# Thirty-two modulation chunks later in a two-block kernel, and two FFN groups that take the contraction by turns

## What is computed

```python
# first block
mod = silu(c) @ w_ada + b_ada                       # 2048 -> 6 * 2048
sh_a, sc_a, gt_a, sh_f, sc_f, gt_f = split(mod, 6)
h = rmsnorm(x, g_pre_attn) * (1 + sc_a) + sh_a
...                                                  # attention on h @ w_in, then w_out
x = x + gt_a * rmsnorm(mix @ w_out, g_post_attn)
h = rmsnorm(x, g_pre_ffn) * (1 + sc_f) + sh_f
f = (silu(h @ w_gate) * (h @ w_up)) @ w_down         # 2048 -> 5632 -> 2048
x = x + gt_f * rmsnorm(f, g_post_ffn)
# second block
shift, scale, gate = split(silu(c_2) @ w_ada_2 + b_ada_2, 3)
h = rms_norm(x, norm1_w) * (1 + scale) + shift
...                                                  # h @ w_in_2, mLSTM, convolution, merged
x = x + gate * (merged @ w_out_2)
return rms_norm(x, normf_w)
```

## Time and profile before

| | |
|---|---|
| median of 3 runs | 2268.4 us (2267.27 to 2268.63) |
| the profiled execution, its own time | 2267.31 us |
| its span | 2265.5 us |
| PE busy | 2235.4 us, 99% |
| DVE busy | 1815.3 us, 80% |
| ACT busy | 1117.6 us, 49% |
| moved by DMA | 598.47 MB, mean 264 GB/s |
| granted clock of PE, mean over the span | 0.998 |

### The profile page before, as it was taken

The page is one execution under the profiler, slowest core; times in us unless marked ns, Lnnn a source line. Parts: engine busy times, 40 slices in busy tenths (PEclk is TensorE's granted clock), DMA queues, the critical chain, the costliest instruction groups (busy, mean ns, idle before and its releaser), DMA issues.

```text
span 2265.5 us, 26257 instructions
## 1 busy us (share of the span) xinstructions
PE 2235.4 (99%) x10314; PEld 1904.2 (84%) x10314; DVE 1815.3 (80%) x2448; ACT 1117.6 (49%) x1473; POOL 14.7 (1%) x31
## 2 busy tenths in 40 slices
PE   9999999999999999999999999999999999999998
PEld 4378888888888888888888888888888888888887
DVE  6788998988889888987675677998878796565885
ACT  5356677564444444544464444444445544454453
POOL 0000000000000000000000000000000000000000
PEclk9999999999999999999999999999999999999999
DMA  9978888888889888898746655556666657655553
GB/s 401 419 291 318 300 341 339 332 319 300 295 318 330 296 296 297 317 352 337 279 164 217 206 209 200 195 200 214 218 218 218 211 197 276 211 202 201 197 205 130
DMA packets 87757, 598.47 MB, mean 264 GB/s; under 512 B 10145, under 2 KB 10209, under 8 KB 16593
## 3 DMA queue, kind: packets, MB, share of 16 engines
q1 hardware_dynamic: 85538, 588.95, 71.2%
q0 software_dynamic: 1664, 7.19, 0.9%
q10 hardware_dynamic: 432, 0.66, 0.1%
HBM read 594.62 MB, written 2.13 MB: 263 GB/s over the span
## 4 chain that ended last, share of the span: by engine, by line
PE 81%; DVE 12%; DMA 3%; issue 2%; ACT 2%; DVEq 0%; ACTq 0%
PE PS L1185 20%; PE PS L1201 16%; PE PS L1210 16%; PE PS L1202 16%; PE PS L1190 10%; DVE LO L1657 4%; DVE RAW L1667 2%; DMA RAW<-in_w_mod 2%; DVE R L1699 2%; DMA RAW<-in_w_first 1%; ACT HI L673 1%; DVE X L1748 0%; PE PS L1362 0%; PE PS L1581 0%; PE PS L1554 0%
## 5 line engine op out<-in xcount | busy, mean ns | idle before, releaser
L673 ACT ACTIVATE HI<-RAW 128x1024 fp32r<-128x1024 f32 x784 | 825.2, 1056 | 991.2 <-PE PS L1210 610.6
L1657 DVE TENSOR_TENSOR LO<-RAW,HI 128x1024 fp32r<-128x1024 f32 x784 | 956.0, 1224 | 368.3 <-ACT HI L673 364.4
L1201 PE MATMUL PS<-HI,XH 128*128 128x512 f32 x2080 | 800.1, 385 | 3.4 <-ACT HI L673 2.4
L1202 PE MATMUL PS<-HI,XL 128*128 128x512 f32 x2080 | 789.3, 379 | 0.0
L1210 PE MATMUL PS<-LO,XH 128*128 128x512 f32 x2080 | 536.6, 380 | 1.5 <-DVE LO L1657 1.4
L1201 PEld LDWEIGHTS PS<-HI,XH 128*128 128x128 f32 x2080 | 393.6, 189 | 62.7 <-DVE XL L1930 3.5
L1210 PEld LDWEIGHTS PS<-LO,XH 128*128 128x128 f32 x2080 | 393.4, 189 | 58.5 <-DVE LO L1657 2.7
L1202 PEld LDWEIGHTS PS<-HI,XL 128*128 128x128 f32 x2080 | 393.7, 189 | 53.7
L1185 PE MATMUL PS<-HI,XH 128*128 128x512 f32 x1056 | 314.8, 380 | 1.9 <-DVE XL L1771 1.3
L1185 PE MATMUL PS<-HI,XL 128*128 128x512 f32 x1056 | 314.1, 379 | 0.0
L1190 PE MATMUL PS<-LO,XH 128*128 128x512 f32 x1056 | 272.7, 379 | 0.0
(11 more groups left out here) (266 smaller groups left out, 895.0 us busy)
## 6 DMA issues: line engine op xcount, KB each, us to landing
RAW<-in_w_second SPq DMA_DIRECT2D x208, 1024.0 KB, 4.9
RAW<-in_w_mod SPq DMA_DIRECT2D x144, 1024.0 KB, 6.0
RAW<-in_w_ffn SPq DMA_DIRECT2D x88, 1024.0 KB, 5.0
RAW<-in_w_first SPq DMA_DIRECT2D x64, 1024.0 KB, 5.8
RAW<-in_w_down SPq DMA_DIRECT2D x44, 1024.0 KB, 5.2
...
R<-mod_rows POOLq DMA_DIRECT2D x3, 1024.0 KB, 7.6
X<-in_x SPq DMA_DIRECT2D x2, 1024.0 KB, 8.6
```

The source lines that it names most:

```text
L673: act.activation(HI[:, (it["half"] + hf) % HLS, :], whole, ACT.Copy).then_inc(s.hi_ready, 1)
L1201: pe.matmul(PS[:, bank + u, :], XH[:, 2 * n + kk, rows], hi, start=start and kk == 0, stop=False)
L1202: pe.matmul(PS[:, bank + u, :], XL[:, 2 * n + kk, rows], hi, start=False, stop=False)
L1657: dve.tensor_tensor(LO[:, slot, :], RAW[:, it["slot"], hf * 1024:(hf + 1) * 1024], HI[:, slot, :].bitcast(F32), ALU.subtract).then_inc(s.l ...
```

## The change

Five things are altered.

1. Eight A are taken out of first: those behind chunks 22, 25, 28, 31, 34, 37, 40 and 43. It holds 68 then; the FFN's shift and scale are ready for pairs 0 to 4 alone when the FFN starts.
2. The FFN's groups 0 and 1 take the contraction by turns: five chunks of group 0, five of group 1, three of group 0, three of group 1. So pairs 5, 6 and 7 are first used at halves 20, 22 and 24. PE transposes pairs 3 to 7 behind halves 2 to 6; ACT copies pairs 5 to 7 from PSUM to SBUF unmodulated (keep_turned, ahead of which stands the copy of halves 8 to 10); their modulation stands at halves 11, 17 and 22. Twelve A, four for each of the three pairs, stand behind the FFN's chunks 1 to 10, two behind chunks 7 and 9. ffn has 40 A in all, down 20.
3. The sixteen A of the last gate are done in second, one behind each of chunks 166 to 181 (halves 332 to 363). For them POOL loads c_2's row into C_ROW once more and ACT takes its silu at half 330.
4. Group 0's evacuation comes at half 29, and its transposes at halves 30 to 37, two to a half.
5. The warm-up matmuls at the start are 22 and 14 small ones (run_warm, 128 columns in float32) in place of 20 and 16 (first_warm, second_warm); the memset of HI for them is gone.

The diff, cut to the core:

```diff
-ADA_BEHIND = list(range(20, 64))
-ADA_ORDER = [*range(62), *range(64, 78), 62, 63, 78, 79, *range(80, 144)]
-ADA_WITH_FFN = 76
+ADA_BEHIND = [c for c in range(20, 64) if c not in range(22, 46, 3)]
+
+LATE_PAIRS = (5, 6, 7)
+ADA_ORDER = [*range(58), *range(64, 74), *(a for n in LATE_PAIRS for a in (48 + 2 * n, 49 + 2 * n, 64 + 2 * n, 65 + 2 * n)),
+             *range(80, 144)]
+ADA_WITH_FFN = 68
+ADA_LAST_GATE = 128
...
+MODULATED_AT = {6: 3, 8: 4, 11: 5, 17: 6, 22: 7}
...
+def ffn_chunks():
+
+    first = [(g, k) for ks in (range(0, 2 * LATE_PAIRS[0], 2), range(2 * LATE_PAIRS[0], NK, 2)) for g in range(2) for k in ks]
+    return first + [(g, k) for g in range(2, 11) for k in range(0, NK, 2)]
...
 def ffn_body():
     body = []
-    for c in range(11 * NK // 2):
-        body.append(("W", c // 8, 2 * (c % 8)))
-        if 5 * c // 11 != 5 * (c + 1) // 11 or c in (1, 3, 40, 42):
+    for c, (g, k) in enumerate(ffn_chunks()):
+        body.append(("W", g, k))
+        body += [("A",)] * (c in range(1, 11)) + [("A",)] * (c in (7, 9))
+        if c > 10 and 28 * (c - 11) // 77 != 28 * (c - 10) // 77:
             body.append(("A",))
...
-        if k < 36 and k % 3:
+        if k < 40 and k % 2:
             body.append(("A",))
+def second_body():
...
+            if 166 <= 4 * g + k // 4 < 182:
+                body.append(("A",))
...
             pool.wait_ge(s.hat_ready, 4)
+            pool.dma_start(NORMF, normf_w_2[None, :].to_broadcast([P, D])).then_inc(s.normf_in, 16)
+            pool.wait_ge(s.group_out, left(PROJ_B - 1))
+            pool.dma_start(C_ROW, c_rows[1:2, :].to_broadcast([P, D])).then_inc(s.c_2_in, 16)
             gate_rows(2, GG2)
-            pool.dma_start(NORMF, normf_w_2[None, :].to_broadcast([P, D])).then_inc(s.normf_in, 16)
...
+            def keep_turned(n):
+
+                no = turn_no(0, n, 0)
+                act.wait_ge(s.pair_t, no)
+                act.activation(as_turned(n), turned_to(0, n, (0, 1)), ACT.Copy).then_inc(s.pair_out, 1)
...
+                late = t == 0 and n in LATE_PAIRS
+                if late:
+                    act.wait_ge(s.mod_ready, 10 + LATE_PAIRS.index(n))
+                    act.wait_ge(s.pair_out, no)
...
-                    if h in (7, 9, 11, 13, 15):
-                        modulate(0, (h - 1) // 2, (0, 1))
+                    if h in MODULATED_AT:
+                        modulate(0, MODULATED_AT[h], (0, 1))
                     if h >= 4:
                         hi_half(sec, 0, it, hf)
...
+                    if h in (8, 9, 10):
+                        keep_turned(h - 3)
...
+                if h == 330:
+                    act.wait_ge(s.c_2_in, 32)
+                    act.activation(C_ROW, C_ROW, ACT.Silu).then_inc(s.cact_ready, 1)
...
-            pe.wait_ge(s.dve_chain, 5)
-            first_warm()
+            run_warm(7, 22)
...
-            second_warm()
+            run_warm(0, 14)
...
-                    if h in (3, 5, 7, 9, 11):
-                        turn_pair(0, (h + 3) // 2, (0, 1), 5 + (h > 3))
+                    if 2 <= h < 7:
+                        turn_pair(0, h + 1, (0, 1), 5 + (h > 2))
...
-                if a == MOD_AT[0] + 31:
-                    modulation(2, 1, 14, 16, ADA_WITH_FFN + 4)
+                for i, n in enumerate(LATE_PAIRS):
+                    if a == MOD_AT[0] + NK + 2 * n + 1:
+                        modulation(2 + i, 1, 2 * n, 2 * n + 2, ADA_WITH_FFN + 4 * i + 4)
```

113 lines of the change are left out of this document (61 added, 52 removed).

## The result

| | before | after |
|---|---|---|
| median of the runs that stood side by side | 2267.84 us (2265.84 to 2268.63, 4 runs) | 2284.0 us (2280.35 to 2285.32, 4 runs) |
| ratio after to before, 95% interval | | 1.0066 (1.0054 to 1.0078) |
| the profiled execution, its own time | 2267.31 us | 2284.29 us |
| its span | 2265.5 us | 2282.5 us |
| granted clock of PE, mean over the span | 0.998 | 0.995 |

The change makes the kernel slower by 0.66%, some 15 us. The prediction had the side right and the size wrong: 2274.6 us, range 2269 to 2279. The change was run a second time in the study (run e5): ratio 1.0059 (1.0046 to 1.0071).

The account below looks back on a forecast made before the run. TensorE (PE), busy for 99% of the span, bounds the kernel, so only waits change. Terms -1.5 + 4.8 + 1.7 + 1.2 = +6.2 us take 2267.3 to 2273.5, median 2274.6; range 2269 to 2279.

Parts of the forecast that it names:

- Term 1: Beside attention: two PE waits for DVE, 1.24 and 0.23 us, go with the A taken out; -1.5 us.
- Term 2: Start of the FFN: DVE's work and round trips with ACT make half 22 start later than 514.77; +4.8 us.
- DVE's list of 51.5 us: FFN's start, ahead of half 22's LO: 12 A, 18 LO, XL of pairs 3 to 6, three modulations.
- the round trips: FFN's start: DVE's modulation, then ACT's pair and HI; 2.0 us for pairs 5 and 6 together, 2.65 for pair 7.
- so they are just hidden: FFN's start: at 422 GB/s the seventeenth load lands at 507.5, half 20 needs it at 509.6; no cost.
- Term 3: PE's clock at the FFN's start: one fall to about half for 3.4 us after a wait; +1.7 us, bounds none or two.
- Term 4: Second block, halves 351 to 369: DVE's work for the last gate outruns its 7.0 us stock; +1.2 us, 0 to 3.
- land late once: Second block, upper bound of 3 us: loads of W and A, two in 5.2 us, come late one time.
- Terms at nothing: Small warm-ups (0 to +1 us), group 0's evacuation, two f_turn to a half, POOL's row, gate_rows: no cost.
- The loads set the pace: Rival, FFN's start: loads at 360 GB/s, half 22 late by 8.1 instead of 4.8; +9.5 in all, 2277.9 us; chance 0.12.

Follow-up runs that it names:

- e4: Smaller version of the change: four A leave first, pairs 6 and 7 late, silu at half 26, last gate's A in down; 2266.05 us, ratio 0.9991.
- e7: Changed kernel, loads of the FFN's first twelve A cut to 512 of 2048 columns, DVE's work whole; 2281.28 us, ratio 1.0053.
- e2: Changed kernel with pair 7's modulation and XL one half later, at half 23; 2280.86 us, ratio 1.0055.
- e6: Changed kernel, DVE taking 64 of 2048 columns of each of the FFN's first twelve A, loads whole; 2275.5 us, ratio 1.0035.
- e9: Changed kernel, the FFN's first twelve A loading 512 columns and DVE taking 64 of them; 2269.65 us, ratio 1.0005.
- e1: Changed kernel with silu of c_2's row behind half 26 of the FFN instead of half 20; 2282.59 us, ratio 1.0059.
- e12: Changed kernel with the last gate's A back in down, silu of c_2's row at half 26, pair 7 at half 23; 2277.27 us, ratio 1.0040.
- e14: Kernel before with only the last gate's sixteen A moved into the second block, their loads cut to 512 of 2048 columns; 2269.06 us, ratio 1.0004.
- e10: Kernel before with the change's small warm-ups alone; ratio 0.9998.

## Why the prediction was wrong in size

**Term 1, beside attention, -1.5.** Right: the same two waits are gone and those of the A behind chunks 29 and 33 still there (0.45 us each). e4 took these away too. That the profile has -1.46 is partly luck, since the start of the FFN moves by over 3 us; it is at 446.9 in the mean of the eight profiles without these A, and at 448.9 in the six with all of them.

**Term 2, start of the FFN, +4.8.** This step failed. It measured 8.0 us of waits (7.4 in e5), and half 22 came 10.5 us later behind DVE's first A than before, not 4.8 (519.5 less 514.77 is in fact 4.7). DVE's list of 51.5 us and the round trips were right: e7 reproduces them, and e2 shows the third round trip on the path. Two things that it gave no time to did cost time.

- The loads: "so they are just hidden". They aren't. With DVE short they cost 4.8 us of waits by themselves (e6), and whole loads bring half 22 another 3.3 to 4.4 us later than e7's small ones. The sum let 17 loads follow one another at full rate from 462.85; in fact a slot is asked for again only when DVE has freed it (chunk 10's at 505.56, right behind the A in that slot), and comes back 7.2 us later, as others are ahead. The rate of 422 GB/s from 41 to 45 us doesn't hold there either. Even with DVE out of the way the engines, 0.98 busy, brought 393 GB/s (e6), and 369 in the change. Chunk 10 landed at 512.7 and not at 507.5. The rival that had the loads at 360 GB/s said 514.4; I gave it 0.12, because I had judged from a stretch of four microseconds. The Trainium skill, "DMA: Bandwidth & Descriptors", Specifications, has about 358 GB/s as one core's share of HBM. No run shows that as a limit (393 and 420 were reached). As a pace for planning it would have come nearer to the loads' arrival than mine: an estimate by it, 462.85 + 5.0 + 16 x 2.93, is 514.7.
- The list of ACT was counted without silu of c_2's row at half 20: 3.2 us ahead of the copy of half 21, which keep DVE idle for 2.94 us in the profile after and 2.23 in e7. Before the change PE did not wait there, and in e9, with both cuts, it waits 0.4 us, so by itself this costs little. e1 takes the idle time away (4.00 to 0.83 us ahead of half 22), and also shows that a stretch short at several places gives back little when one is mended.

**Term 3, the clock, +1.7.** Too small: two falls behind the waits, 10.2 us at half clock, 4.5 to 5.1 us lost (e5: one of 6.8, 3.4 lost). It rests on term 2. In this stretch all seven waits of 2.78 us or more (after, e2, e5, e6, e7, e12) had half clock for 3.4 or 6.8 us with them, starting from 1.3 us ahead of the wait's end to 1.4 behind it; of those of 1.6 to 2.5 us two had (e1) and five had not (e2, e5 twice, e6, e12), and none of those below 1.2. In the seven profiles with the twelve A and waits at halves 14 to 23 (e9's 0.4 us left out), halves 12 to 26 lose about half to three quarters as much again as the waits, so a forecast of waits alone leaves out a third or more of the price. The third fall in after, right behind the join, has no wait of the change ahead of it; the unchanged waits at the join were followed by one in some executions and not in others.

**Term 4, last gate in the second block, +1.2 (0 to 3).** The side was right, the size too small by a factor of nearly three: 4.4 us between halves 350 and 400 in the profile after, 3.3 in the mean of the eight profiles that have it as the change does. The waits came at halves 362 and 364, not at 365 to 369. The step that failed is that the sum took DVE's list alone and let late loads come in only as an upper bound, "land late once". With small loads the term is 1.4 (e14), near the 1.2 of the list; with whole ones it is two to two and a half times that. That DVE's lateness makes the loads late, and these DVE, is my reading of the two cuts and of ACT's waits for loads there (4.43 and 2.94 us).

**Terms at nothing.** The warm-ups: right (e10). Group 0's evacuation at half 29, the two f_turn to a half, POOL's row and gate_rows: PE waited for none of them. That 44 + 24 A became 40 + 20 won nothing, right (from half 26 on ffn and down keep the pace of before).

**Rivals.** "The loads set the pace", +9.5, came nearest in time and had chunk 10's arrival nearly right, but loads alone are not what happened: e7, which takes most of them away, keeps most of the waits. I had no case in which both are short at once, and that is the one that came. The sum of what was measured in the profile after: -1.46 up to the first join, 1.11 at it, 13.42 between halves 12 and 26 (8.0 of waits, the rest mostly clock) and 3.93 from the second join on, 17.0 together.

**What stays open.** The part of each cause in the waits of a single execution can't be told, since which half waits changes from run to run. How much whole loads add to DVE's list at the FFN's start is not settled either, as e7's profile and its median disagree. That the DMA rate is 369 to 393 and not 420 GB/s in this stretch was measured but not explained. Other places for the two A that stand as second ones behind chunks 7 and 9, or a fifth slot, were not tried; nor was either cut run with silu at half 26.
